# Reordering the joined work of three mixers in a two-block transformer kernel, and computing the memory's row norm once

## The chip, the cores and the metric

One NeuronCore of a Trainium2 chip runs the whole program. The metric is device time in microseconds (us) of one execution, as the median of several. Engines are named as the profile names them: PE is TensorE (its weight loads are PEld), DVE is VectorE, ACT is ScalarE, POOL is GpSimd, and SP issues the weight DMAs.

## The reference

256 tokens of width 1024 go through two blocks one after the other. Cut to what matters here (norm scales, rotary tables and shapes are left out):

```python
# first block: layer 0, then layer 1
x = x + 0.5 * swiglu(rmsnorm(x) , up, down)          # "ffn0"
qkv, z, b, a, rq, rk, rv, rg = split(rmsnorm(x) @ w_in)      # "in0", 14 panels of weights
qkv = silu(causal_depthwise_conv(qkv, conv_w))       # conv, four taps
o = concat(gated_delta_rule(qkv, ...), retention(rq, rk, rv))
x = x + o @ w_out                                    # "out0", then ffn1
x = x + 0.5 * swiglu(...)                            # ffn2
h = rmsnorm(x) @ w_in                                # "in1", 12 panels
o = concat(dilated_attention(4 heads "dil"), softmax(s1) - lam * softmax(s2), 4 heads "dif")
x = x + o @ w_out                                    # "out1", then ffn3, final norm
# second block: two layers l of the same form
for l in range(2):
    kv_m = (rms_norm(mem) * mem_norm_g[l]) @ w_mem_kv[l]     # "mem0", "mem1": same mem in both
    q_a, k_a, v_a, q_h, f_h, i_h, q_m, z = split(rms_norm(x) @ w_in[l])   # "in2_l", 20 panels
    o_a = moba_attention(q_a, k_a, v_a)              # 8 heads "moba"
    o_h = hgrn2(q_h, log_f(f_h), i_h)                # gated recurrence
    o_m = memory_attention(q_m, k_m, v_m)            # 4 heads "matt"
    x = x + (concat(o_a, o_h, o_m) * silu(z)) @ w_out[l]     # "out2_l"
```

## The kernel before

All weights stream through the core once, as panels of 128 x 2048 numbers (1 MB). SP loads panel n into one of three slots of `raw`. ACT copies it, rounded, to `w_hi` (`split_hi(n)`, line 1512) and DVE takes the rest, raw minus `w_hi`, to `w_lo` (`split_lo(n)`, line 1827). PE then multiplies the panel in three products of parts (lines 1010 to 1012), which land in one of two PSUM banks, and an "evacuate" copies them out: on DVE (line 1940) for the first 12 panels of `in0`, else on ACT (line 1612 or 1609). Panel k of an input projection may start when panel k-2 has been evacuated and when its own `split_lo` is done. A slot's `split_hi(n)` waits until PE has used panel n-3.

Every engine works strictly in order. The order is written out by hand: `order()` returns one list of steps (engine, kind, arguments), and each engine runs its own steps of it. `rounds(steps, units)` makes a software pipeline (each step with a lag in rounds), `merge` lays several of them side by side, and `weave(chain, pieces, places)` puts half panels between the rounds at the rounds that a list of places names. In a woven stretch a panel comes as two halves: PE `half(name, k, 0)` and `(name, k, 1)`, ACT `half_hi` (line 1521), DVE `half_lo` (line 1810).

The three places that the change touches:

- First mixer. `in0` panels 0 to 5 feed the convolution. Per panel p: PE product, DVE evacuate, ACT `tap(p)` (line 1629, the first tap), DVE `conv(p-1)` (line 1953, three taps, six instructions), ACT `conv_silu(p-2)` (line 1635), `split_hi` and `split_lo` of the panel three further on. Panel 1 has with it the small products for the gates (`ab_exp`, `softplus`, `g`). Then come the woven rounds of the delta rule: `cumsum`, `gc` (DVE line 1973), `gap` (1980), `decay`, and norms over columns (`cn_sq` on ACT line 1702, `cn_sum` on PE line 1406, `cn_rstd` on ACT line 1710, `cn_use` on DVE line 2078 or 2080). The places are `BESIDE_0`.
- Attention heads. Each head is a pipeline: `scores` on PE (lines 1419, 1421), `mask_max` on DVE (2114), `exp` on ACT (1721), `divide` on DVE (2131, 2135), `turn_p` on PE (transposes, 1431 to 1437), `p_cols` on ACT (1732), `attend` on PE (1377, 1378). `mask_max` of head i waits for `scores(i)` and for `turn_p(i-2)`, whose buffer it writes; `turn_p(i)` waits for `divide(i)`. Two lists fix the order inside a round: `ATTEND_TWO` has `turn_p` ahead of `scores`, `SCORES_FIRST` the reverse. The second mixer (heads dif 0 to 3, dil 0 to 3, woven with `in1` panels 8 to 11) uses the first, the two last mixers use the second.
- Last mixers (`last_mixer(l)`). `f_abs`, `f_ln`, `f_log` and, in layer 1 only, `f_ln2`, `f_log2` (DVE lines 2197, 2198) make the log decay; `k_gate` (ACT 1765) and `cum_f` (DVE 2203) follow, then `diagonal` (PE 1262) and eight levels. Two column norms of the memory keys (`sk`) run beside them. Places are `BESIDE_2`, counted from round n. During layer 0's heads the memory is loaded again (`mem1`), ACT takes its row statistics (`sumsq`, `row_rstd`, lines 1553 to 1561) and DVE scales the rows (`scale`, line 1905).

Of the kernel before, what the change touches and what calls it, by code (L numbers as in the profile page):

```python
# [241 lines left out]
BESIDE_0 = [0, 0, 0, 0, 0, 2, 3, 4, 5, 5, 8, 10, 12, 14, 16, 18]  # L242
# [133 lines left out]
def hgrn_rounds(l):  # L376

    out = [[("dve", "f_abs", (l,)), ("act", "f_ln", (l,))], [("dve", "f_log", (l,))]]
    if l:
        out += [[("act", "f_ln2", (l,)), ("dve", "f_log2", (l,))]]  # L380
    out += [[("act", "k_gate", (l,)), ("dve", "cum_f", (l,))], [("pe", "diagonal", (l,)), ("dve", "diagonal_in", (l,))]]
    ahead = len(out)
    for r in range(8 + 2):
        out.append([(e, k, (l, v)) for e, k, v in
                    [("dve", "gap_f", r), ("act", "decay_f", r), ("dve", "q_level", r - 1), ("pool", "k_level", r - 1),
                     ("pe", "level", r - 2), ("dve", "level_in", r - 2)] if 0 <= v < 8])
    return out + [[("pe", "hgrn_out", (l, g)) for g in (0, 1)]], ahead


def last_mixer(l):  # L390
# [13 lines left out]
    if l == 0:  # L404
        load, *stats = mem_norm(1)
        chains += [[[]] * (h + 1) + [[load]] + [[]] * 3 + [[s for s in stats if s[0] == "act"]] +
                   [[s for s in stats if s[1] == "scale"]]]
    if l:
        chains += [[[]] * (h + 7) + sum(([[("pe", "turn_back", (b,)), ("act", "rows_back", (b,))], []] for b in range(PAIRS)), [])]
    places = [n + r for r in BESIDE_2]  # L410
    out = weave(merge(*chains), halves(panel_list(f"in2_{l}", None, 4)), places)
# [38 lines left out]
def order():  # L450
# [12 lines left out]
    for p, (product, evacuate, *late) in enumerate(panel_list("in0", None, 0, 6)):  # L463
# [3 lines left out]
        out += [evacuate, ("act", "tap", (p,))]  # L467
# [3 lines left out]
        out += [("dve", "conv", (p - 1,))][:p] + ([("act", "conv_silu", (p - 2,))] if p > 1 else []) + late  # L471
    out += [("dve", "conv", (5,)), ("act", "conv_silu", (4,)), ("act", "conv_silu", (5,)), ("act", "logs", ())]
    out += weave(delta_rounds(), halves(panel_list("in0", None, 6)), BESIDE_0)
# [11 lines left out]
    heads = rounds(ATTEND_TWO, [("dif", h) for h in range(4)] + [("dil", h) for h in range(4)])  # L485
# [47 lines left out]
def at(engine, kind, *args):  # L533

    return COUNT_AT[engine, kind, args]


def build(nc, x_in, mem_in, pos_in, panels, gains, small_in, tab0, tab1, tab2, tab3, out):
    with ExitStack() as ctx:
# [1241 lines left out]
        def _(dve):  # L1781
# [121 lines left out]
            def scale(tag, t):  # L1903
                dve.wait_ge(act_done, at("act", "row_rstd", tag, t))
                finish(ts(rows_of(tag)[:, t], rows_of(tag)[:, t], rstd[:, t:t + 1], None, ALU.mult))
# [422 lines left out]
```

## Time and profile before

| | |
|---|---|
| runs | 1621.41, 1624.90, 1620.96 us, median 1621.41 |
| profiled execution | 1623.86 us, of which the span of the trace is 1621.9 |
| PE busy | 1545.7 us, 95% |
| DVE busy | 1177.0 us, 73% |
| ACT busy | 768.9 us, 47% |
| mean granted clock of PE | 0.974 of 2.4 GHz |
| DMA | 246.76 MB, mean 152 GB/s |

How to read it: a timeline row gives the start, the time from start to end, engine, line, operation, output and inputs, and how many instructions of the kind stand there in a row. In square brackets stands how long the engine was idle before the first of them, and which instruction ended that idle time. In windows of time the columns are the stretch, its length, then busy time and count for PE, PEld, DVE, ACT, POOL, then the granted clock as a share of 2.4 GHz, DMA share and GB/s.

### The profile page before, as it was taken

How to read it: one execution, taken by the hardware profiler on the slowest of the kernel's cores; microseconds unless marked ns; L12 is line 12 of the kernel's file. 1: busy time of each engine (PE TensorE's matmuls, PEld its weight loads, DVE VectorE, ACT ScalarE, POOL GpSimd, SP SyncE). 2: the span in 40 equal slices, each digit the busy share in tenths (PEclk: the TensorE clock that was granted, in tenths of full speed). 3: DMA queues.
4: the chain of work that ended last, by engine and by line, in shares of the span. 5: the costliest groups of instructions: out<-in, count | busy, mean ns of one | idle time of the engine just before them, and what ended most of it. 6: DMA issues, size and time to landing. Idle time of an engine off the chain costs nothing.

```text
span 1621.9 us, 23947 instructions
## 1 busy us (share of the span) xinstructions
PE 1545.7 (95%) x9974; PEld 1370.5 (84%) x9974; DVE 1177.0 (73%) x1391; ACT 768.9 (47%) x943; POOL 94.1 (6%) x66
## 2 busy tenths in 40 slices
PE   7999997998999999999997999999999999899998
PEld 6888897887888888888886888888999579799857
DVE  7888667636887788786676787867787565589654
ACT  5333545315433454334535533355646554544653
POOL 1000000010000000000000100001021001013000
PEclk9999999999999999999999999999999789999979
DMA  7555533204555555555431555554443224434202
GB/s 278 201 189 183 179 133 130 79 27 161 204 185 183 185 177 186 203 182 182 173 113 59 202 202 185 182 182 156 156 161 126 78 86 175 156 108 153 104 1 78
DMA packets 51888, 246.76 MB, mean 152 GB/s; under 512 B 4619, under 2 KB 5771, under 8 KB 27718
## 3 DMA queue, kind: packets, MB, share of 16 engines
q1 hardware_dynamic: 50662, 238.29, 42.0%
q0 software_dynamic: 1120, 6.96, 1.2%
q8 instruction: 79, 1.29, 0.3%
q14 instruction: 27, 0.22, 0.0%
HBM read 244.18 MB, written 1.05 MB: 151 GB/s over the span
## 4 chain that ended last, share of the span: by engine, by line
PE 75%; DVE 13%; ACT 6%; issue 3%; DVEq 0%; POOL 0%; ACTq 0%
PE ps L1059 18%; PE ps L1061 9%; PE ps L1010 9%; PE ps L1012 8%; PE ps L1011 8%; PE ps L1111 7%; PE ps L1262 4%; PE ps L1112 4%; DVE w_lo L1827 3%; ACT w_hi L1512 2%; PE ps L1406 1%; DVE act_two L1933 1%; PE ps L1377 1%; ACT act_two L1590 1%; DVE x L1890 1%
## 5 line engine op out<-in xcount | busy, mean ns | idle before, releaser
L1827 DVE TENSOR_TENSOR w_lo<-raw,w_hi 128x2048 fp32r<-128x2048 f32 x188 | 437.2, 2331 | 151.9 <-ACT w_hi L1512 149.3
L1512 ACT ACTIVATE w_hi<-raw 128x2048 fp32r<-128x2048 f32 x188 | 358.9, 1912 | 389.9 <-PE ps L1061 274.9
L1059 PE MATMUL ps<-act_two,w_hi 128*128 128x512 f32 x1408 | 443.9, 397 | 5.0 <-DVE w_lo L1827 2.4
L1010 PE MATMUL ps<-act_two,w_hi 128*128 128x256 f32 x1120 | 331.2, 296 | 18.6 <-DVE act_two L1933 5.4
L1011 PE MATMUL ps<-act_two,w_hi 128*128 128x256 f32 x1120 | 320.0, 286 | 0.0
L1012 PE MATMUL ps<-act_two,w_lo 128*128 128x256 f32 x1120 | 319.9, 286 | 0.0
L1061 PEld LDWEIGHTS ps<-act_two,w_lo 128*128 128x128 f32 x1408 | 264.9, 188 | 62.9
L1061 PE MATMUL ps<-act_two,w_lo 128*128 128x256 f32 x1408 | 277.0, 278 | 0.0
L1010 PEld LDWEIGHTS ps<-act_two,w_hi 128*128 128x128 f32 x1120 | 218.1, 195 | 26.2 <-issue 9.0
L1059 PEld LDWEIGHTS ps<-act_two,w_hi 128*128 128x128 f32 x1408 | 214.9, 189 | 8.0 <-DVE w_lo L1827 3.6
L1011 PEld LDWEIGHTS ps<-act_two,w_hi 128*128 128x128 f32 x1120 | 218.3, 195 | 3.5 <-issue 3.4
L1012 PEld LDWEIGHTS ps<-act_two,w_lo 128*128 128x128 f32 x1120 | 217.9, 195 | 0.0
L1111 PE MATMUL ps<-g_two,w_hi 128*128 128x512 f32 x384 | 136.2, 398 | 0.0
L1810 DVE TENSOR_TENSOR w_lo<-raw,w_hi 128x1024 fp32r<-128x1024 f32 x72 | 98.9, 1403 | 24.2 <-ACT w_hi L1521 23.1
L1111 PE MATMUL ps<-act_two,w_hi 128*128 128x512 f32 x320 | 113.4, 398 | 3.1 <-DVE act_two L1866 2.5
L1112 PE MATMUL ps<-g_two,w_lo 128*128 128x256 f32 x384 | 107.5, 280 | 0.0
L1010 PE MATMUL ps<-w_hi,act_two 128*128 128x256 f32 (+1 forms) x336 | 106.8, 318 | 0.0
L1011 PE MATMUL ps<-w_lo,act_two 128*128 128x256 f32 (+1 forms) x336 | 100.6, 299 | 0.0
L1012 PE MATMUL ps<-w_hi,act_two 128*128 128x256 f32 (+1 forms) x336 | 100.5, 299 | 0.0
L994 POOL TENSOR_TENSOR pair<-pair 128x512 f32<-128x512 f32 x27 | 41.1, 1520 | 872.6 <-ACT pair L1569 871.9
L1112 PE MATMUL ps<-act_two,w_lo 128*128 128x256 f32 x320 | 89.5, 280 | 0.0
L1111 PEld LDWEIGHTS ps<-g_two,w_hi 128*128 128x128 f32 x384 | 72.1, 188 | 16.9
(282 smaller groups left out, 2059.8 us busy)
## 6 DMA issues: line engine op xcount, KB each, us to landing
raw<-panels SPq DMA_DIRECT2D x184, 1024.0 KB, 4.8
raw<-panels SPq DMA_DIRECT2D x80, 512.0 KB, 4.8
raw<-panels SPq DMA_DIRECT2D x8, 256.0 KB, 6.3
table<-tab POOLq DMA_DIRECT2D x1, 1472.0 KB, 9.4
table<-tab POOLq DMA_DIRECT2D x1, 1216.0 KB, 5.6
xn<-x_in SPq DMA_DIRECT2D x4, 256.0 KB, 5.0
work<-mem_in POOLq DMA_DIRECT2D x1, 1024.0 KB, 9.5
xn<-mem_in POOLq DMA_DIRECT2D x1, 1024.0 KB, 5.4
```

The source lines that it names most:

```text
L994: nc.gpsimd.tensor_tensor(pair[:, 0:512], pair[:, 0:512], pair[:, 512 * b:512 * b + 512], ALU.add).then_inc(pool_done, 1)
L1010: pe.matmul(o, l[0], r[0], start=start, stop=False, skip_group_check=shared)
L1011: pe.matmul(o, l[0], r[1], start=False, stop=False, skip_group_check=shared)
L1012: return pe.matmul(o, l[1], r[0], start=False, stop=stop, skip_group_check=shared)
L1059: pe.matmul(grid(ps[:, bank + half], 2), w[half][0], act_two[:, slots[c]], start=c == 0, stop=False)
L1061: ins = pe.matmul(ps[:, bank + half, 0:SEQ], w[half][1], act_hi[:, slots[c]], start=False, stop=c == DC - 1)
L1111: pe.matmul(grid(ps[:, bank], 2), hi, two, start=first and m == 0, stop=False)
L1112: ins = pe.matmul(ps[:, bank, 0:SEQ], lo, two[:, 0], start=False, stop=last and m == len(quarters) - 1)
L1262: ins = pe.transpose(oh, lhs(h), ident) if turn else pe.matmul(oh, lhs(h), rhs(h), start=True, stop=True)
L1512: nc.scalar.activation(w_hi[:, s], raw[:, s], ACT.Copy).then_inc(panel_hi, 1)
L1810: ins = tt(w_lo[:, s, c], raw[:, s, c], w_hi[:, s, c].bitcast(F32), ALU.subtract)
L1827: tt(w_lo[:, s], raw[:, s], w_hi[:, s].bitcast(F32), ALU.subtract).then_inc(panel_lo, 1)
```

## The change

It edits the order of steps and drops some instructions; no product of the reference is computed otherwise.

```diff
-BESIDE_0 = [0, 0, 0, 0, 0, 2, 3, 4, 5, 5, 8, 10, 12, 14, 16, 18]
+BESIDE_0 = [0, 0, 1, 2, 2, 4, 5, 6, 7, 7, 10, 12, 14, 16, 18, 20]
...
     if l:
-        out += [[("act", "f_ln2", (l,)), ("dve", "f_log2", (l,))]]
+        out += [[], [("act", "f_ln2", (l,)), ("dve", "f_log2", (l,))]]
...
     if l == 0:
         load, *stats = mem_norm(1)
-        chains += [[[]] * (h + 1) + [[load]] + [[]] * 3 + [[s for s in stats if s[0] == "act"]] +
-                   [[s for s in stats if s[1] == "scale"]]]
+        chains += [[[]] * (h + 1) + [[load]] + [[]] * 4 + [[s] for s in stats if s[1] == "scale"]]
...
     places = [n + r for r in BESIDE_2]
+    if l:
+        places[:4] = [0, 1, 2, 2]
...
-        out += [evacuate, ("act", "tap", (p,))]
+        his, los = [[x for x in late if x[0] == e] for e in ("act", "dve")]
+        out += [evacuate] + his + [("act", "tap", (p,))]
...
-        out += [("dve", "conv", (p - 1,))][:p] + ([("act", "conv_silu", (p - 2,))] if p > 1 else []) + late
-    out += [("dve", "conv", (5,)), ("act", "conv_silu", (4,)), ("act", "conv_silu", (5,)), ("act", "logs", ())]
-    out += weave(delta_rounds(), halves(panel_list("in0", None, 6)), BESIDE_0)
+        out += [("dve", "conv", (p - 1,))][:p] + ([("act", "conv_silu", (p - 2,))] if p > 1 else []) + los
+    conv_end = [[], [], [("dve", "conv", (5,)), ("act", "conv_silu", (4,)), ("act", "conv_silu", (5,)), ("act", "logs", ())]]
+    out += weave(conv_end + delta_rounds()[1:], halves(panel_list("in0", None, 6)), BESIDE_0)
...
-    heads = rounds(ATTEND_TWO, [("dif", h) for h in range(4)] + [("dil", h) for h in range(4)])
+    heads = rounds(SCORES_FIRST, [("dif", h) for h in range(4)] + [("dil", h) for h in range(4)])
...
             def scale(tag, t):
-                dve.wait_ge(act_done, at("act", "row_rstd", tag, t))
+
+                dve.wait_ge(act_done, at("act", "row_rstd", "mem0", t))
+                dve.wait_ge(loaded[tag], 16)
```

What this does to each engine's own order:

- First mixer, ACT: `split_hi(36)` to `(41)`, six of them, each go ahead of `tap(p)` (and so of `ab_exp`, `softplus` and `conv_silu(p-2)`), and `half_hi(42, 0)` goes ahead of `conv_silu(4)`.
- First mixer, DVE: the evacuation of `in0` panel 6 and `half_lo(42, 0)` go ahead of `conv(5)`.
- Second mixer, PE: `scores` of dif 2, dif 3 and dil 0 to 3, six heads, go ahead of the `turn_p` of the head two before.
- Last mixer of layer 1, PE: `half(in2_1, 4, 0)` goes ahead of the first `cn_sum`. ACT: the evacuation of panel 4 and both `half_hi(207)` go ahead of `f_ln2`, the evacuation of panel 5 and `half_hi(208, 0)` ahead of `k_gate`. DVE: both `half_lo(207)` go ahead of `f_log2`, and `half_lo(208, 0)` ahead of `cum_f`.
- Last mixer of layer 0: `sumsq` and `row_rstd` of `mem1` are gone from ACT (14 records of it in the trace). The two `scale` steps read the root that `mem0` left, and stand in two rounds and no longer in one.

On DVE, at the end of the convolution, the order before (first row: evacuation of panel 5, then `conv(4)`, `split_lo(41)`, `conv(5)`, evacuation of panel 6, halves of panel 42, evacuation of panel 7, halves of 43, `gc`):

```order
L1940 TENSOR_TENSOR work<-ps,r_b 128x2x256
L1953 SCALAR_TENSOR_TENSOR work<-work,small 128x256 x6
L1827 TENSOR_TENSOR w_lo<-raw,w_hi 128x2048
L1953 SCALAR_TENSOR_TENSOR work<-work,small 128x256 x6
L1940 TENSOR_TENSOR work<-ps,r_b 128x512
L1810 TENSOR_TENSOR w_lo<-raw,w_hi 128x1024 x2
L1940 TENSOR_TENSOR work<-ps,r_b 128x512
L1810 TENSOR_TENSOR w_lo<-raw,w_hi 128x1024 x2
L1973 COPY stat<-ps 128x8
```

The same place on DVE with the change (line numbers of the changed file are 2 to 4 higher):

```order
L1944 TENSOR_TENSOR work<-ps,r_b 128x2x256
L1957 SCALAR_TENSOR_TENSOR work<-work,small 128x256 x6
L1829 TENSOR_TENSOR w_lo<-raw,w_hi 128x2048
L1944 TENSOR_TENSOR work<-ps,r_b 128x512
L1812 TENSOR_TENSOR w_lo<-raw,w_hi 128x1024
L1957 SCALAR_TENSOR_TENSOR work<-work,small 128x256 x6
L1812 TENSOR_TENSOR w_lo<-raw,w_hi 128x1024
L1944 TENSOR_TENSOR work<-ps,r_b 128x512
L1812 TENSOR_TENSOR w_lo<-raw,w_hi 128x1024 x2
L1977 COPY stat<-ps 128x8
```

The evacuation of panel 6 and the first half of panel 42 have moved past the last `conv`.

On PE, in the heads of the second mixer, before: after the last product of `half(in1, 9, 1)` come `turn_p` of dif 0 (three transposes), then `scores` of dif 2 (two maps of two products), then the next half panel:

```order
L1012 MATMUL ps<-w_hi,act_two 128x256
L1431 MATMUL ps<-const,work 128x128
L1432 MATMUL ps<-const,work 128x128
L1437 MATMUL ps<-const,work 128x128
L1419 MATMUL ps<-work 128x128
L1421 MATMUL ps<-work 128x256
L1419 MATMUL ps<-work 128x128
L1421 MATMUL ps<-work 128x256
L1010 MATMUL ps<-w_hi,act_two 128x256
```

With the change, at the same place on PE:

```order
L1014 MATMUL ps<-w_hi,act_two 128x256
L1421 MATMUL ps<-work 128x128
L1423 MATMUL ps<-work 128x256
L1421 MATMUL ps<-work 128x128
L1423 MATMUL ps<-work 128x256
L1433 MATMUL ps<-const,work 128x128
L1434 MATMUL ps<-const,work 128x128
L1439 MATMUL ps<-const,work 128x128
L1012 MATMUL ps<-w_hi,act_two 128x256
```

The two steps have changed places, here and at five heads more.

On ACT, in the last mixer of layer 1, before: `cn_rstd` of the second key norm (Ln, Exp), `f_ln2` (Exp, Ln), evacuation of panel 4, halves of 207, `k_gate`, evacuation of panel 5, halves of 208:

```order
L1710 ACTIVATE pair<-ps,const 128x512
L1711 ACTIVATE pair<-pair 128x512
L1760 ACTIVATE work<-work 128x1024
L1761 ACTIVATE work<-work,const 128x1024
L1612 ACTIVATE work<-ps 128x2x256
L1521 ACTIVATE w_hi<-raw 128x1024 x2
L1765 ACTIVATE work<-work 128x1024
L1612 ACTIVATE work<-ps 128x2x256
L1521 ACTIVATE w_hi<-raw 128x1024 x2
```

With the change, from the same `cn_rstd` on ACT:

```order
L1712 ACTIVATE pair<-ps,const 128x512
L1713 ACTIVATE pair<-pair 128x512
L1614 ACTIVATE work<-ps 128x2x256
L1523 ACTIVATE w_hi<-raw 128x1024 x2
L1762 ACTIVATE work<-work 128x1024
L1763 ACTIVATE work<-work,const 128x1024
L1614 ACTIVATE work<-ps 128x2x256
L1523 ACTIVATE w_hi<-raw 128x1024
L1767 ACTIVATE work<-work 128x1024
L1523 ACTIVATE w_hi<-raw 128x1024
```

The evacuation of panel 4 no longer stands behind `f_ln2`, and that of panel 5 not behind `k_gate`.

## Rows read from the trace of the kernel before

**Rows 1.** The page, part 1: busy time of PE.
```profile
PE 1545.7 (95%) x9974; PEld 1370.5 (84%) x9974; DVE 1177.0 (73%) x1391; ACT 768.9 (47%) x943; POOL 94.1 (6%) x66
```
**Rows 2.** Groups of DVE, 232 to 256 us (group, busy, mean ns, idle before it).
```profile
L1827 DVE TENSOR_TENSOR w_lo<-raw,w_hi 128x2048 fp32r<-128x2048 f32 x4 | 9.2, 2292 | 4.6 <-ACT w_hi L1512 4.6
```
**Rows 3.** Timeline of DVE, end of the first mixer's convolution.
```profile
256.36 2.71 DVE L1953 SCALAR_TENSOR_TENSOR work<-work,small 128x256 f32<-128x256 f32 x6
259.11 0.69 DVE L1940 TENSOR_TENSOR work<-ps,r_b 128x512 f32<-128x512 f32 x1
262.30 2.36 DVE L1810 TENSOR_TENSOR w_lo<-raw,w_hi 128x1024 fp32r<-128x1024 f32 x2 [2.50 <-ACT w_hi L1521]
...
267.57 0.16 DVE L1973 COPY stat<-ps 128x8 f32<-128x8 f32 x1
```
**Rows 4.** Timeline of ACT, the three half panels before the first column norm.
```profile
261.14 2.95 ACT L1521 ACTIVATE w_hi<-raw 128x1024 fp32r<-128x1024 f32 x3
```
**Rows 5.** Timeline of PE, first mixer, its two long waits.
```profile
259.85 0.39 PE L1010 MATMUL ps<-act_two,w_hi 128*128 128x256 f32 x1 [3.18 <-DVE work L1940]
...
273.46 1.22 PE L1406 MATMUL ps<-pair,const 128*128 128x512 f32 x1 [4.51 <-ACT pair L1702]
```
**Rows 6.** Timeline of DVE, `mask_max` of dil 1 and dil 2.
```profile
867.98 0.29 DVE L2114 CUSTOM_DVE_ANT_0 work<-ps,table 128x128 f32<-128x128 f32 x1 [1.39 <-PE ps L1421]
...
872.50 0.29 DVE L2114 CUSTOM_DVE_ANT_0 work<-ps,table 128x128 f32<-128x128 f32 x1 [2.40 <-PE ps L1421]
```
**Rows 7.** Timeline of PE, `scores` of dil 2.
```profile
871.54 0.39 PE L1419 MATMUL ps<-work 128*128 128x128 f32 x2
```
**Rows 8.** Timeline of PE, first product of `out1`.
```profile
885.68 0.39 PE L1010 MATMUL ps<-act_two,w_hi 128*128 128x256 f32 x1 [1.48 <-DVE act_two L2071]
```
**Rows 9.** Timeline of ACT, first and last of 14 records of `mem1`'s statistics.
```profile
1292.39 0.63 ACT L1553 ACTIVATE work<-xn 128x512 f32<-128x512 f32 x1
...
1297.24 0.20 ACT L1561 ACTIVATE stat<-stat 128x1 f32<-128x1 f32 x1
```
**Rows 10.** Timeline of DVE, `cn_use` behind them.
```profile
1298.78 0.75 DVE L2078 SCALAR_TENSOR_TENSOR work<-work,small,pair 128x512 f32<-128x512 f32 x1 [6.74 <-ACT pair L1711]
```
**Rows 11.** Timeline of PE, `turn_p` of moba 5, layer 0 and layer 1.
```profile
1301.05 0.48 PE L1431 MATMUL ps<-const,work 128*128 128x128 f32 x1 [1.68 <-DVE work L2131]
...
1565.57 0.47 PE L1431 MATMUL ps<-const,work 128*128 128x128 f32 x1
```
**Rows 12.** Windows of both last mixers.
```profile
1304.00:1308.00 4.00, 4.00 (x16) 2.58 (x15) 1.53 (x8) 1.71 (x7) 0.00 (x0) 0.75 0.00 0
1429.75:1438.23 8.48, 8.48 (x48) 8.48 (x49) 8.38 (x10) 5.29 (x6) 0.00 (x0) 0.65 0.34 122
1439.93:1445.72 5.79, 5.79 (x51) 5.79 (x50) 4.85 (x6) 1.58 (x3) 0.00 (x0) 1.00 0.64 201
1440.00:1540.00 100.00, 100.00 (x796) 95.09 (x796) 81.39 (x87) 52.78 (x66) 19.39 (x8) 1.00 0.39 137
```
**Rows 13.** Timeline of PE, last mixer, layer 1: both `cn_sum`, first products of two halves.
```profile
1411.42 0.84 PE L1406 MATMUL ps<-pair,const 128*128 128x512 f32 x1 [4.43 <-ACT pair L1702]
...
1419.70 1.02 PE L1406 MATMUL ps<-pair,const 128*128 128x512 f32 x2
...
1429.75 0.58 PE L1010 MATMUL ps<-act_two,w_hi 128*128 128x256 f32 x1 [3.29 <-ACT work L1612]
...
1439.93 0.37 PE L1010 MATMUL ps<-act_two,w_hi 128*128 128x256 f32 x1
```
**Rows 14.** Timeline of ACT there: `cn_sq` of the second key norm, `k_gate`.
```profile
1417.02 0.61 ACT L1702 ACTIVATE pair<-work 128x512 f32<-128x512 f32 x1
...
1431.84 1.06 ACT L1765 ACTIVATE work<-work 128x1024 f32<-128x1024 f32 x1 [0.24 <-DVE work L2198]
```
**Rows 15.** Timeline of DVE there: `cn_use`, first half of `f_log2`.
```profile
1426.98 0.75 DVE L2078 SCALAR_TENSOR_TENSOR work<-work,small,pair 128x512 f32<-128x512 f32 x1
1429.32 1.23 DVE L2197 TENSOR_TENSOR work<-work,stat 128x1024 f32<-128x1024 f32 x1 [1.58 <-ACT work L1761]
```

## The prediction

> **What bounds the kernel now.** I read the page's busy times first: PE is busy 95% of the span and every other engine well below it [rows 1]. So a step that moves on DVE or ACT is worth only the PE idle time that it takes away, and PE has about 76 us of it. Then I went through windows and the timeline of PE for its waits near the four places that the diff edits, and from each wait to the engine that ended it. The reader should see, at each place, who comes last: in the first mixer DVE's evacuation and later ACT's norm [rows 5]; at the end of the second mixer the chain of heads, since `out1` can't start before it [rows 8]; in layer 0's last mixer DVE's `divide` [rows 11]; in layer 1's last mixer ACT, twice [rows 13]. Behind the last of these DVE is busy 81 of 100 us and PE all 100 [rows 12], so what PE gains up to there stays gained, and nothing more is won behind it.
>
> **First mixer.** Per panel DVE has conv 2.71, split_lo 2.3 and the evacuation 0.69 [rows 2, 3], 5.7 us, against about 5.8 us of PE products (48 products at full clock took no more than 5.79 in a window [rows 12]). Yet DVE waits 4.6 us in four pieces for `split_hi` [rows 2], which stands behind `tap(p)`, and `tap(p)` waits for DVE's own evacuation. With `split_hi` ahead, these waits go. Against it: `split_hi(37)` now also stands ahead of `ab_exp`, and the first conv starts later: by at least nothing and at most the 1.9 that two halves of a split take on ACT [rows 4]; I take the middle, 1.0, since ACT has idle time there too. So `split_lo(41)`, which ended at 256.36, ends 3.6 earlier, at 252.8. The evacuation of panel 6 comes right there, at 252.9 and no longer at 259.11 [rows 3]: PE's wait of 3.18, which it ended [rows 5], goes in full, since PE was free at 256.67. `conv(5)` has that evacuation (0.7) and a half_lo (1.2) put ahead of it: it starts at 254.8, 1.6 before. Behind its silu ACT has two halves and no longer three before `cn_sq`, 1.0 less [rows 4]: 2.6 earlier. DVE has one half_lo of 1.2 less between `conv(5)` and `gc` [rows 3]: 2.8. What ends PE's second wait (4.51 [rows 5]) comes that much earlier, while that wait keeps its size, for PE arrives earlier too. Behind it PE does the same work. Gain **2.8**; if ACT's silus decide and not the halves, 1.6.
>
> **Second mixer.** In a dil head PE's `scores` take 0.96 us from their start at 871.54 to `mask_max` at 872.50 [rows 6, 7], and they stand behind `turn_p`, which waits for `divide`, which DVE does just ahead of its wait. So they lie on a loop DVE to PE to DVE. DVE waits 1.39, 2.40 and once more 1.39 for them (dil 1 to 3) [rows 6]. With `scores` ahead, `mask_max` waits for `turn_p` alone: 0.9 less each time. But in the 2.40 PE is the late one, with half panels between; it is earlier only by what the loop before gave. I count 0.9 for dil 1, none for dil 2, 0.8 for dil 3: `out1`'s first product, at 885.68 after a wait [rows 8], comes **1.7** earlier. Bounds: 0.8 (one loop) and 2.7 (three). The early heads give nothing: their DVE stands behind half panels.
>
> **Last mixer, layer 0.** The 14 records of statistics hold ACT 5.0 us, 1292.39 to 1297.44 [rows 9]. `cn_rstd` stands behind them, DVE's `cn_use` waits 6.74 for it [rows 10], and PE then 1.68 for `divide` at `turn_p` of moba 5. In layer 1, where ACT has no statistics, the same `turn_p` has no wait [rows 11]. So 1.68 goes; the rest of the 5 us is slack of PE. The clock is 0.75 over 1304 to 1308 [rows 12], so 1.0 us is still lost there. If it rises earlier with the work, up to 1.0 more is won; if it rises when it did, part of the work pulled forward runs at half speed and 0.8 of the gain is lost. Taken **2.0**, range 0.9 to 2.6. Loading and scaling the rows without statistics costs nothing: the two scales stand on DVE before as well.
>
> **Last mixer, layer 1.** PE waits 4.43 before the first `cn_sum` and 3.29 before the next panel's halves [rows 13]. (a) `half(4, 0)`, some 3.1 us (15.04 from 1411.42 to 1426.46 hold four halves and both `cn_sum`), moves into the 4.43. The first `cn_sum` stays, since ACT ends it. The second, at 1419.70, would come at 1416.6, but needs `cn_sq`, which ACT does at 1417.02 to 1417.63 [rows 14]: a new wait of 1.0 to 1.2, gain 2.1. (b) PE is then free at 1424.3 and the next halves' bank, whose evacuation stood behind `f_ln2`, is free by then: no wait of 3.29. They end at 1424.3 + 5.8 = 1430.1 (before, 1438.23). (c) Then comes `diagonal`, which needs the decay. DVE now has two half_lo (2.36 [rows 3]) ahead of `f_log2`: `cn_use` at 1426.98 (0.75), they to 1430.09, `f_log2` with its two halves of 1.23 [rows 15] to 1432.5, against 1431.6 when `k_gate` at 1431.84 had waited 0.24 for it [rows 14]. So `k_gate` ends at 1433.65, 0.7 later, and `diagonal` starts there. The first product behind it, now 1439.93, 1.7 behind `diagonal`'s start at 1438.23, comes at 1435.4: 4.5 earlier. PE has a **new wait of 3.6** before `diagonal`. (d) The clock. Behind the old wait of 3.29 it stood at 0.65 for 8.48 us, and 48 products took 8.48 where 5.79 is the time at 1.00 [rows 12]: 2.7 lost. The new wait of 3.6 may do the same. Behind the 3.18 in the first mixer the first product took 0.39, as in warm stretches, not 0.58 [rows 5, 13]. Waits of one size went both ways, so I take back 1.6, between 0 and 2.7. Gain **2.9**.
>
> On (d), the Trainium skill, "TensorE: Matmul & The Clock Gate", section "HAM oscillation — how this bites in real kernels", says that idle gaps between bursts of matmuls let the clock gate throttle PE again and that each restart costs cold work. The old wait of 3.29 and the 0.65 behind it agree; the 3.18 does not. By the page alone (d) would give 4.5 − 2.7 = 1.8, by the 3.18 row 4.5.
>
> **Sum.** 2.8 + 1.7 + 2.0 + 2.9 = 9.4. The profiled execution took 1623.86 and would become 1614.5. It lies 2.45 above the median of the three runs, so against that median, 1621.41, the time is **1612.0**.
>
> **The rivals.**
> B: both clock terms go the bad way, 1.8 in place of 2.9 and 0.9 to 1.2 in place of 2.0: sum 7.3, 1614.1. For it speaks the old wait of 3.29, against it the 3.18.
> C: no clock is lost behind the new wait (4.5) and the heads of layer 0 bring their 2.6: sum 11.6, 1609.8.
> D: the change doesn't do what it says at two or more places: the late arrivals are replaced by ones just behind them (in the first mixer silu and table load: 1.6; heads 0.8; layer 0 0.9; layer 1, where the 3.6 costs its clock and `k_gate` comes later than I work out, 1): sum 4.3, 1617.1, within 0.3%. Against it: PE's waits of 3.18, 1.68 and 3.29 each have one releaser that plainly moves.
> E, slower. ACT works in order, and `split_hi(36)` to `(41)`, now ahead of `tap`, `ab_exp` and `conv_silu`, must wait for their slot of `raw`, which PE and the load free and fill. In the old order each stood behind a wait for the evacuation, which covered that. If each of six is late, ACT's `tap`, then `conv`, then the next evacuation slip with it. To lose what the rest brings, and to be 0.3% slower, it must cost 14 us, 2.4 per panel. Nothing in the rows shows DVE or ACT waiting for a load there; the four waits of DVE name ACT, not a queue [rows 2].
>
> **How the numbers follow.** 0.3%, 4.9 us, is about what can be told from no change. Chances: forecast (1610.5 to 1613.5) 0.50, B 0.20, C 0.17, D 0.10, E 0.03. B and C are both faster by more than 4.9 us, as is the forecast: faster 0.87; D is the same; E slower. The range runs from 1607.5 (C with the second mixer at 2.7, which is 1608.8, and 1.3 more for the spread of the runs, which is 3.9 from end to end) to 1617.0 (D just reached).
>
> **What would show it.** First mixer: no idle PE before `half(8, 0)`; its later wait still some 4.5, 2.8 earlier; DVE without waits for `split_hi`. If these are there with loads as releasers, E is at work. Second mixer: `mask_max` of the dil heads waits for `turn_p` only. Layer 0: `turn_p` of moba 5 without idle, DVE's wait 6.74 about halved. Layer 1: a short wait before the second `cn_sum`, none before the halves of panel 6, 3.6 before `diagonal`; the granted clock behind it decides between the forecast, B and C. The prediction is wrong if DVE stands at `f_log2` later than 1432.5, if the clock stays down longer than 8.5 us behind the new wait, or if PE's wait in the first mixer only moves from the evacuation to the second one.

## The result, and the profile after

The changed kernel took 1608.06, 1608.75, 1607.84 and 1603.33 us, median 1607.95, against 1621.41 before; the ratio is 0.9907, 95% interval 0.9887 to 0.9926. That is 15 us (12 to 18) faster, where 9.4 were forecast: the direction was right, the size too small. 0.9907 of 1621.41 is 1606.3, below the low end of the range, 1607.5; the plain median, 1607.95, lies just inside it.

The page of the changed kernel, busy times (the same number of products on PE, so less busy time means products at a higher clock):

```profile
PE 1534.8 (96%) x9974; PEld 1364.8 (85%) x9974; DVE 1176.8 (73%) x1391; ACT 765.3 (48%) x929; POOL 94.0 (6%) x66
```

PE is busy 10.9 us less than in [rows 1], in a span that is 16.0 shorter (1605.9). So only 5.1 us came out of PE's idle time, and two thirds came from the same products running faster: the granted clock was low for 84 us of the trace before and for 59 of this one. The forecast was a sum of idle times, with no more than 1.6 us for the clock in any term.

Windows of the changed kernel, then of the one before, cut so that PE has the same work in each (the counts behind PE's busy time agree within 4). The four stretches are all up to the heads of layer 0; those heads; up to the heads of layer 1; the rest:

```profile
0.00:1270.00 1270.00, 1221.69 (x7880) 1094.10 (x7881) 956.61 (x1033) 588.51 (x643) 66.09 (x50) 0.99 0.48 166
1270.00:1320.00 50.00, 44.64 (x224) 30.20 (x224) 32.25 (x103) 29.02 (x74) 0.58 (x1) 0.86 0.13 45
1320.00:1520.00 200.00, 191.44 (x1525) 184.67 (x1523) 142.09 (x143) 108.55 (x129) 25.15 (x11) 0.99 0.42 147
1520.00:1605.00 85.00, 77.05 (x351) 55.84 (x349) 45.83 (x115) 39.22 (x85) 2.23 (x4) 0.90 0.13 50
```
```profile
0.00:1272.00 1272.00, 1221.53 (x7880) 1093.25 (x7881) 956.38 (x1033) 587.96 (x643) 66.12 (x50) 0.99 0.48 166
1272.00:1328.40 56.40, 50.18 (x225) 32.77 (x225) 32.26 (x103) 33.03 (x88) 0.58 (x1) 0.76 0.11 41
1328.40:1531.40 203.00, 192.41 (x1521) 186.42 (x1520) 141.19 (x142) 108.07 (x128) 25.14 (x11) 0.97 0.41 145
1531.40:1621.00 89.60, 81.54 (x354) 58.01 (x352) 47.20 (x116) 39.80 (x85) 2.23 (x4) 0.86 0.13 47
```

The first 1272 us, with the first and second mixer in them, gave 2.0 us; the heads of layer 0, 50 us long, gave 6.4.

The first mixer, DVE of the changed kernel, answering to [rows 3]:

```profile
255.68 2.71 DVE L1957 SCALAR_TENSOR_TENSOR work<-work,small 128x256 f32<-128x256 f32 x6
261.62 1.23 DVE L1812 TENSOR_TENSOR w_lo<-raw,w_hi 128x1024 fp32r<-128x1024 f32 x1 [3.23 <-ACT w_hi L1523]
...
265.76 0.16 DVE L1977 COPY stat<-ps 128x8 f32<-128x8 f32 x1
```

This execution was 0.9 us late before the mixer began (at 200 us it is 0.88 behind, and one stretch of 3.4 us at half clock lies at 27 to 31). So `conv(5)` came at 254.8 and `gc` at 264.9 on the old scale: 2.7 earlier, as worked out. PE's waits there, answering to [rows 5]:

```profile
263.04 1.12 PE L1408 MATMUL ps<-pair,const 128*128 128x512 f32 x2 [1.49 <-ACT pair L1704]
271.65 2.08 PE L1408 MATMUL ps<-pair,const 128*128 128x512 f32 x2 [4.63 <-ACT pair L1704]
```

The wait of 3.18 is gone, one of 1.49 for the column norm stands in its place, and the second keeps its size: 4.51 in the trace before.

`mask_max` of dil 1, 2 and 3 on DVE, answering to [rows 6], and `out1`, answering to [rows 8]:

```profile
867.38 0.29 DVE L2118 CUSTOM_DVE_ANT_0 work<-ps,table 128x128 f32<-128x128 f32 x1 [0.78 <-PE ps L1439]
871.88 0.29 DVE L2118 CUSTOM_DVE_ANT_0 work<-ps,table 128x128 f32<-128x128 f32 x1 [2.40 <-PE ps L1439]
874.77 0.29 DVE L2118 CUSTOM_DVE_ANT_0 work<-ps,table 128x128 f32<-128x128 f32 x1 [0.78 <-PE ps L1439]
```
```profile
884.45 0.56 PE L1012 MATMUL ps<-act_two,w_hi 128*128 128x256 f32 x1 [1.48 <-DVE act_two L2075]
```

They wait for `turn_p` now, 0.6 less at dil 1 and 3 (1.39 before at both) and the same 2.40 at dil 2: `out1` starts 1.23 earlier. At 845 us, ahead of these heads, the two traces stand at the same product at the same time, so the 1.23 is theirs.

The heads of layer 0, PE at `turn_p` of moba 5, answering to [rows 11], and two windows:

```profile
1295.14 0.33 PE L1433 MATMUL ps<-const,work 128*128 128x128 f32 x1 [0.79 <-DVE work L2135]
```
```profile
1277.60:1291.00 13.40, 13.22 (x33) 6.61 (x33) 4.95 (x23) 7.36 (x21) 0.00 (x0) 0.51 0.00 0
1291.00:1305.00 14.00, 13.21 (x64) 8.07 (x64) 9.95 (x39) 9.11 (x27) 0.00 (x0) 1.00 0.00 1
```

And the stretch at half clock of the kernel before:

```profile
1278.80:1305.90 27.10, 24.72 (x63) 12.80 (x62) 10.65 (x44) 16.33 (x50) 0.00 (x0) 0.50 0.03 14
```

Before, 63 products took 24.7 us of PE at 1.2 GHz; now PE is at 2.4 GHz from 1291 on and does 64 in the next 14 us. The prediction had named no idle time at `turn_p` of moba 5; 0.79 is left.

Layer 1's last mixer, PE, answering to [rows 13]:

```profile
1403.07 1.12 PE L1408 MATMUL ps<-pair,const 128*128 128x512 f32 x2 [1.55 <-ACT pair L1704]
1409.33 1.29 PE L1408 MATMUL ps<-pair,const 128*128 128x512 f32 x2 [2.27 <-ACT pair L1704]
...
1425.32 2.05 PE L1264 MATMUL ps<-work 128*128 128x128 f32 x16 [1.85 <-ACT work L1767]
...
1427.12 0.37 PE L1012 MATMUL ps<-act_two,w_hi 128*128 128x256 f32 x1
```

From the first `cn_sum` to the first product behind `diagonal` it is 24.05 us, before 28.51: 4.5 less. `diagonal` itself comes 22.25 behind `cn_sum`; 22.2 had been worked out (1433.65 less 1411.42).

### The profile page after: what moved, and what is told of

It reads as the page before. It is cut to its first block, busy times and chain, and to the rows that moved or that the text cites. A ratio compares the mean times of both kernels' runs of the same rounds, so it can differ in the third digit from the quotient of the medians.

```text
span 1605.9 us, 23931 instructions
## 1 busy us (share of the span) xinstructions
PE 1534.8 (96%) x9974; PEld 1364.8 (85%) x9974; DVE 1176.8 (73%) x1391; ACT 765.3 (48%) x929; POOL 94.0 (6%) x66
## 4 chain that ended last, share of the span: by engine, by line
PE 78%; DVE 13%; ACT 5%; issue 2%; DMA 0%; SPq 0%; DVEq 0%; POOL 0%; ACTq 0%
PE ps L1061 19%; PE ps L1063 10%; PE ps L1012 9%; PE ps L1014 9%; PE ps L1013 9%; PE ps L1113 7%; PE ps L1264 4%; PE ps L1114 4%; DVE w_lo L1829 3%; ACT w_hi L1514 2%; PE ps L1408 1%; DVE act_two L1937 1%; PE ps L1379 1%; ACT act_two L1592 1%; DVE x L1892 1%
## 5 line engine op out<-in xcount | busy, mean ns | idle before, releaser
L1812 DVE TENSOR_TENSOR w_lo<-raw,w_hi 128x1024 fp32r<-128x1024 f32 x72 | 98.7, 1397 | 25.1 <-ACT w_hi L1523 23.9
```

Of the source, the lines that this page charges most:

```text
L1812: ins = tt(w_lo[:, s, c], raw[:, s, c], w_hi[:, s, c].bitcast(F32), ALU.subtract)
```

## The experiments

Two theories. **Idle**: each part gives the idle time that it takes from PE, and the surplus is the clock's chance. **Floor**: the statistics on ACT set a least length for the heads of layer 0, whatever PE's clock did, so that their removal gives the idle time and also makes an early rise of the clock worth something.

Half-clock time below is summed from windows of 1 us of each trace. The kernels were timed in series, each with the kernel before beside them, and means are compared inside a series. Over all 111 executions the kernel before had a mean of 1621.0 us, from 1614.4 to 1626.7, with a standard deviation of 3.3; its means by series ran from 1618.7 to 1622.3. The standard error of a difference of means inside a series is 0.7 to 1.7 us.

**Each part alone, on the kernel before.** The edits are the hunks of the diff: `first_only` has those of `BESIDE_0` and the first mixer, `second_only` this one,

```diff
-    heads = rounds(ATTEND_TWO, [("dif", h) for h in range(4)] + [("dil", h) for h in range(4)])
+    heads = rounds(SCORES_FIRST, [("dif", h) for h in range(4)] + [("dil", h) for h in range(4)])
```

`root_only` those of `mem_norm(1)` and `scale`, `last_only` the round of `f_ln2` and `places`.

first_only: 

> The kernel before with the first mixer's part alone (split_hi ahead of tap, the joined order at the end of the convolution, BESIDE_0). Theory 1, idle time removed: PE's wait of 3.18 us before half(8, 0) goes, the place behind it comes 2.8 to 3.0 us earlier, and the whole kernel is 2.8 us faster (ratio 0.998). Theory 2, clock: of these 3 us about 2 are given back between 340 and 420 us, where the changed kernel had 10.2 us at half clock and the one before 6.8; the whole is 1 us faster (0.9994), and the two long half-clock stretches of the last mixers (27.3 and 23.9 us before) change although nothing of this part stands there.

second_only: 

> The kernel before with the second mixer's part alone (scores ahead of turn_p in six heads). Theory 1: out1 starts 1.2 to 1.7 us earlier, the whole 1.2 to 1.7 faster (ratio 0.999). Theory 2: the same at out1, and then a change of 3 to 7 us in either direction at the last mixers' half-clock stretches, since the work there only falls at another time.

root_only: 

> The kernel before without the second statistics of the memory. Theory 1: PE's 1.68 us wait before turn_p of moba 5 goes, the half-clock stretch there stays about 27 us, gain 1.7 to 2.6 us (ratio 0.9986). Theory 2a, this part itself shortens the stretch: it ends before 1300 us and the gain at that place is 5 to 7 us (0.9965). Theory 2b, the stretch is shorter only because the work before it came 2 us earlier: it stays at 27 us here.

last_only: 

> The kernel before with layer 1's part of the last mixer alone (f_ln2 and f_log2 a round later, first four places 0, 1, 2, 2). Theory 1: the first product behind diagonal comes 2.9 to 4.5 us earlier, nothing is lost to the clock behind the new 3.6 us wait before diagonal, and the whole is 2.9 to 4.5 faster (ratio 0.9977). Theory 2: 4.5 at diagonal, and the stretch at half clock in layer 1's heads (23.9 us before, 17.1 in the changed kernel) is shorter by multiples of about 3.4, each worth 1.7 us, so 4.5 to 8 in all (0.996).

| kernel | ratio (95%) | mean, less the mean before | what its place shows |
|---|---|---|---|
| first_only | 0.9987 (0.9972 to 1.0003) | -2.1 | gc 2.7 earlier |
| second_only | 0.9980 (0.9963 to 0.9997) | -3.6 | out1 1.2 earlier |
| root_only | 0.9953 (0.9930 to 0.9975) | -7.5 | heads of layer 0 3.0 shorter |
| last_only | 0.9969 (0.9953 to 0.9984) | -5.6 | first product behind diagonal 4.5 earlier than before's profile |

At their places the first, second and last part give the same as in the changed kernel. The statistics' part gives the most in the whole (-7.5, standard error 1.7). Its own trace had the clock low for 23.9 us in those heads, so that there theory 2a was not seen and the place gave 3.0, with no wait at `turn_p` of moba 5:

```profile
1298.42 0.47 PE L1430 MATMUL ps<-const,work 128*128 128x128 f32 x1
```

The traces with the statistics show why the mean is larger. `turn_p` of moba 5 in `first_only`, in `second_only` and in `last_only`:

```profile
1298.28 0.48 PE L1432 MATMUL ps<-const,work 128*128 128x128 f32 x1 [6.27 <-DVE work L2132]
```
```profile
1295.67 0.47 PE L1431 MATMUL ps<-const,work 128*128 128x128 f32 x1 [6.58 <-DVE work L2131]
```
```profile
1302.15 0.47 PE L1433 MATMUL ps<-const,work 128*128 128x128 f32 x1 [4.71 <-DVE work L2133]
```

In these three the clock had risen early, at about 1286, 1283 and 1294. The reader is to see the wait: 6.27, 6.58 and 4.71 in place of 1.68 in [rows 11]. From `turn_p` of moba 0 (1275.09, 1272.41, 1278.66; before 1277.56) it is 23.2, 23.3, 23.5 and 23.5 us, nearly the same each time, with PE at 1.2 or at 2.4 GHz; three more traces that kept the single statistics (`half_only`, `round_only`, `stats_back`, below) have 23.2, 23.5 and 23.2. Without the statistics it was 21.7 with the clock low throughout (`root_only`) and 19.6 in the changed kernel. And during the long wait the clock fell again in these three traces, for 6.8 us.

**The statistics put back, doubled in time, and moved.** `stats_back` is the changed kernel with the third part undone. `stats_twice` adds to it eight more sums of squares, 5.0 us of ACT:

```diff
+                if tag == "mem1":
+                    for _ in range(2):
+                        step(nc.scalar.activation(mem_squares[tag][:, 512 * i:512 * i + 512], rows_of(tag)[:, t, c], ACT.Square, accum_out=sumsq[:, i:i + 1]))
```

`stats_spread` is the kernel before, all the work kept, one step in a round:

```diff
-        chains += [[[]] * (h + 1) + [[load]] + [[]] * 3 + [[s for s in stats if s[0] == "act"]] +
-                   [[s for s in stats if s[1] == "scale"]]]
+        chains += [[[]] * (h + 1) + [[load]] + [[]] * 3 + [[s] for s in stats if s[0] == "act"] +
+                   [[s] for s in stats if s[1] == "scale"]]
```

`changed_again` is the changed kernel once more.

changed_again: 

> The changed kernel once more, to have its mean and that of the kernel before over many executions, and a second trace. Both theories: 1605 to 1608 us, ratio 0.991. Clock by chance: the half-clock stretches in the heads of both layers (13.6 and 17.1 us in the first trace) come out differently by multiples of 3.4 us, although the kernel is the same. Clock set by the program: the same stretches again.

stats_back: 

> The changed kernel with the memory's statistics put back into layer 0's heads (the third part undone). Floor theory: with the 14 records on ACT the time from turn_p of moba 0 to turn_p of moba 5 is 23.2 to 23.5 us whatever the clock does (it was in four traces with them; 21.7 and 19.5 in the two without), an early rise of the clock only makes PE's wait there longer (4.7 to 6.6 us) and brings a second drop; the whole is 5 to 7 us slower than the changed kernel. Theory of one wait: only PE's 1.7 us come back, 2 us slower. Clock by chance: no difference beyond 1.7 us in the mean over the runs.

stats_twice: 

> The changed kernel with the statistics put back and each of their four sums of squares taken three times, 8 more ACT instructions of 0.63 us, 5.0 us more in the same place. The output is the same. Floor theory: turn_p of moba 0 to moba 5 takes 28.3 us, 5.0 more than with the single statistics, one for one. If PE at half clock were the bound of that stretch: 5.0 minus what is slack, about 3.

stats_spread: 

> The kernel before with the statistics kept, but spread over six rounds of the heads, one instruction group in each, and the two scales in rounds of their own. Floor theory, place of the work: no long ACT block stands ahead of cn_rstd, the stretch from moba 0 to moba 5 takes 19 to 22 us as without them, and the kernel is as fast as with the statistics dropped (root_only, 0.9953, within 0.002). Theory of the amount of work: only leaving the 5 us of ACT work out helps, and the ratio stays at 0.999 to 1.000.

| kernel | ratio (95%) | mean | moba 0 to moba 5, layer 0 |
|---|---|---|---|
| changed_again | 0.9906 (0.9888 to 0.9924) | 1605.5 | 19.7 |
| stats_back | 0.9953 (0.9935 to 0.9971) | 1613.1 | 23.2 |
| stats_twice | 0.9987 (0.9974 to 1.0001) | 1618.3 | 29.3 |
| stats_spread | 0.9968 (0.9948 to 0.9987) | 1615.2 | 19.7 |

`turn_p` of moba 5 in `stats_back`, `stats_twice` and `stats_spread`:

```profile
1295.50 0.48 PE L1434 MATMUL ps<-const,work 128*128 128x128 f32 x1 [6.34 <-DVE work L2134]
```
```profile
1302.19 0.47 PE L1434 MATMUL ps<-const,work 128*128 128x128 f32 x1 [10.48 <-DVE work L2137]
```
```profile
1296.47 0.33 PE L1431 MATMUL ps<-const,work 128*128 128x128 f32 x1 [0.79 <-DVE work L2131]
```

The floor stands: back, the statistics cost 7.6 us of mean, and the floor is again 23.2. With 5 us more in the same place it is 6.1 longer (a little over one for one), and 5.2 in the mean. Spread out, the same ACT work leaves PE only the 0.79 of the changed kernel: it was the block in one place ahead of `cn_rstd`, not the work. In the whole `stats_spread` is 5.2 faster than the kernel before by means, `root_only` 7.5; the two do not differ beyond their uncertainty. The half-clock stretches of the changed kernel came out as in the first trace (13.6 and 17.1 us), and a third trace, `changed_third` below, has them again. That does not rule out chance: the two traces of one other kernel, `log_first` and `log_first_again` below, have 13.6 and 10.2, then 10.2 and 17.1.

**The last part in pieces.** `half_only` is the kernel before with `places[:4] = [0, 1, 2, 2]` alone, `round_only` with this alone:

```diff
-        out += [[("act", "f_ln2", (l,)), ("dve", "f_log2", (l,))]]
+        out += [[], [("act", "f_ln2", (l,)), ("dve", "f_log2", (l,))]]
```

half_only: 

> The kernel before with the list of places alone changed in layer 1 (half(4, 0) ahead of the first cn_sum), f_ln2 and f_log2 left in their round. Theory, both pieces are needed: the wait of 4.43 us before cn_sum is filled, but the evacuation of panel 4 still stands behind f_ln2 on ACT, so PE's later wait of 3.3 us grows to about 5.5, diagonal starts 26 to 27 us after the first cn_sum as before, gain 0 to 0.5 us. Theory, the filled wait alone is the gain: 2 to 3 us faster.

round_only: 

> The kernel before with f_ln2 and f_log2 alone put a round later, the places unchanged. Theory, both pieces are needed: PE has both cn_sum with no half panel between, so that it waits 4.4 and then up to 5 us for cn_sq, but none for the evacuation of panel 4; diagonal comes 1 to 2 us earlier than before. Theory, the evacuation alone is the gain: 3.3 us faster.

`half_only`: ratio 1.0017 (1.0004 to 1.0030). `round_only`: 0.9996 (0.9985 to 1.0008). PE's wait for the evacuation in the first, and for the second `cn_sq` in the other:

```profile
1429.65 0.58 PE L1012 MATMUL ps<-act_two,w_hi 128*128 128x256 f32 x1 [3.70 <-ACT work L1614]
```
```profile
1418.43 1.22 PE L1406 MATMUL ps<-pair,const 128*128 128x512 f32 x1 [4.50 <-ACT pair L1702]
```

Either piece alone takes one wait and makes another; `diagonal` comes 26.8 and 26.5 us behind the first `cn_sum`, before 26.8. Only together do they give anything; `half_only` is even slower, by 2.0 us in the mean (standard error 0.7).

**Full-size products in the heads.** `fill2` and `fill4` hold half panels of the changed kernel back into the heads:

```diff
-            -1, 0, 1, 2, 3, 4, 5, 6]
+            -1, 0, 1, 2, 3, 4, 7, 8]
```

and `-1, 0, 1, 2, 6, 7, 8, 9]` for `fill4`.

fill2: 

> The changed kernel with the last two half panels of each last mixer held back two rounds, into the first two rounds of the heads. Theory, waits at the head of the heads drop the clock (1.47, 0.94 and 0.81 us within 8 us, then 13 to 17 us at half clock): full-size products between them fill these waits, the half-clock stretches shrink by half or more in both layers, and it is 3 to 8 us faster than the changed kernel. Rival, the small products of the heads hold the clock down whatever stands before them: the same stretches, gain 0 to 2. Rival, the norms that the halves covered now stand bare: 2 to 4 slower.

fill4: 

> The same with the last four half panels held back, to one round ahead of the heads and their first three rounds. Theory of the waits: as fill2 or 1 to 3 us better. Bare norms: 3 to 6 us slower than the changed kernel, since four rounds of norms then have no half panel.

`fill2`: ratio 0.9904 (0.9885 to 0.9924), mean 15.6 below the kernel before beside it, where the changed kernel is 14.2 below in its own series together: 1.4 better with a standard error of 1.6, no gain that can be told. `fill4`: 0.9971 (0.9960 to 0.9982), mean 4.4 below, so some 10 us slower than the changed kernel. In layer 1 the half-clock stretch of `fill2` shrank from 17.1 us to 3.4, all half-clock time from 58 to 32 us (the two other traces of the changed kernel have 49 and 63 in all). In layer 0 it was 10.2 in place of 13.6, which other traces have without the filling. So full-size products between the waits went with a higher clock in layer 1, in one trace; that this pays is not borne out. The rival's waits appeared too, here in `fill4` in layer 0:

```profile
1285.98 0.62 PE L1379 MATMUL ps<-work 128*64 128x256 f32 x2 [2.75 <-ACT work L1614]
```

**Each part left out of the changed kernel, and one step more.** `first_back`, `second_back` and `last_back` undo one part each. `log_first` puts `f_log2` ahead of both `half_lo(207)` on DVE:

```diff
+    if l:
+        i = min(i for i, s in enumerate(out) if s[1] == "half_lo" and s[2][0] == 207)
+        out.insert(i, out.pop(out.index(("dve", "f_log2", (l,)))))
```

first_back: 

> The changed kernel with the first mixer as before. Places theory: 2.7 us slower than the changed kernel, all of it before gc; mean 1608.5 to 1609.5 against 1606. Clock theory: the 3 us shift moves half-clock stretches in or out behind it, any result from 0 to 5 slower.

second_back: 

> The changed kernel with the second mixer's heads as before. Places theory: 1.2 us slower than the changed kernel, at out1. Clock theory: 3 to 4 us slower, as the part alone made the kernel before 3.6 faster in the mean.

last_back: 

> The changed kernel with layer 1's last mixer as before. Places theory: 2.9 us later at the first gap and 4 us later behind the last level, 4 slower in all, 1610; and if more, in the heads of layer 1 that follow, 5 to 6 slower.

log_first: 

> The changed kernel with f_log2 put ahead of both half_lo(207) on DVE. Theory: f_log2 starts when f_ln2 ends, 0.8 us earlier, k_gate and diagonal 0.8 earlier, PE's wait of 1.85 falls to 1.05; the whole 0 to 0.8 us faster than the changed kernel. Rival: half_lo(207), now 3.9 us later, holds up a later load or half panel and nothing is gained, or 1 us lost.

| kernel | ratio (95%) | mean, less the mean before | cost of leaving it out |
|---|---|---|---|
| first_back | 0.9923 (0.9906 to 0.9941) | -12.1 | 2.1 |
| second_back | 0.9931 (0.9913 to 0.9949) | -10.9 | 3.3 |
| last_back | 0.9937 (0.9914 to 0.9959) | -10.1 | 4.1 |
| stats_back, from above | 0.9953 (0.9935 to 0.9971) | -7.4 | 7.6 |
| log_first | 0.9902 (0.9884 to 0.9919) | -15.6 | -1.4 |

The changed kernel is 15.2, 14.9 and 12.8 below the kernel before in its three series, 14.2 by all 16 executions, and the last column is against that (`stats_back` against `changed_again` of its own series). Its standard error is 1.3 to 1.7 us, for `stats_back` 0.8. No changed kernel was timed in the series of the other four, and there the kernel before had its lowest mean, 1618.7; plain differences to the changed kernel's mean of 1606.3 would come out some 2 us smaller (0.3, 1.5, 2.3 and -3.3).

The four left-out parts sum to 17.1 us, the four alone to 18.8, together they are 14.2. Each part has the same order of size both ways, and no pair differs by more than 1.5 us, which is within its uncertainty.

`log_first` did at its place what was worked out:

```profile
1422.20 1.05 PE L1267 MATMUL ps<-work 128*128 128x128 f32 x7 [1.14 <-ACT work L1770]
```

`diagonal` is 0.7 us nearer to the first `cn_sum` (21.5 for 22.25), and the wait 1.14 for 1.85. Beside the changed kernel, in one series:

log_first_again: 

> log_first once more, beside the changed kernel. If its 0.7 us at diagonal is all: its mean is 0 to 1 us below the changed kernel's. If the first comparison holds: 2 to 4 below.

changed_third: 

> The changed kernel, for the comparison with log_first_again in the same call: mean 1605 to 1607 us, and a third trace of its half-clock stretches (13.6 and 17.1 us in the heads in the first two).

`log_first_again`: 0.9917 (0.9896 to 0.9939), mean 1605.9. `changed_third`: 0.9924 (0.9904 to 0.9944), mean 1606.6. The difference is 0.7 us, the size of its place, with a standard error of 0.6. So a gain of 0.7 fits, and none is excluded.

**The places over all traces.** Every trace holds the same 9974 products of PE, so each product of one trace can be found in another and the lag between them followed along the kernel. The table says how much shorter than in the first trace of the kernel before a stretch of products was, in traces with a part and in traces without it (mean, and from least to most; us; the stretches are those of the trace before). Traces in which that place had an edit of its own are left out.

| part | stretch | with it | without it | difference |
|---|---|---|---|---|
| first mixer | 200 to 340 | 3.3 (2.7 to 4.0), 12 traces | 1.2 (0.0 to 2.4), 8 | 2.0 |
| second mixer | 845 to 1000 | 1.7 (1.1 to 3.0), 12 | 0.9 (0.0 to 1.8), 8 | 0.9 |
| no statistics | 1270 to 1328 | 6.3 (2.9 to 7.6), 9 | 0.3 (0.0 to 0.7), 7 | 6.0 |
| last mixer, layer 1 | 1330 to 1460 | 4.3 (3.0 to 4.5), 10 | 1.0 (0.0 to 2.6), 6 | 3.4 |

The third row is the floor once more. Of its seven traces with the statistics, two had the clock low for 27.3 us and five had it rise early, and the stretch was the same to 0.7 us. Of the twelve traces without the block in that place (`fill2`, `fill4` and `stats_spread` too), all but `root_only` had the early rise. The four differences sum to 12.3 us, by standard errors of 0.3 to 0.5 each, against 14.2 in the mean of all executions.

## Why the prediction was wrong

**First mixer, 2.8: right where it was read, less behind it.** Up to the end of PE's second wait it is about 2.7 in every trace that has this part. Of what was named, only the place of PE's remaining wait differs (1.49 before a `cn_sum`). Behind it the gain is 2.0 on average, and some 2 us in the whole (2.1 alone, 2.1 when left out). The cause is the old order: in the first trace the clock stayed up behind the wait of 3.18 and PE then waited 4.51; in the seven other traces of the old order it fell there, and the second wait was 2.2 to 3.0, so that less was lost in total. The clock of the stretch with the 3.18 in it, in the first trace, in `root_only` and in `first_back`, and the second wait in `root_only`:

```profile
255.00:265.00 10.00, 6.82 (x58) 6.61 (x58) 7.39 (x11) 5.87 (x8) 0.00 (x0) 1.00 0.29 107
```
```profile
255.00:265.00 10.00, 6.83 (x45) 6.63 (x44) 7.39 (x11) 6.07 (x8) 0.00 (x0) 0.83 0.31 106
```
```profile
255.00:265.00 10.00, 6.82 (x38) 6.62 (x37) 7.39 (x11) 6.12 (x8) 0.00 (x0) 0.67 0.30 106
```
```profile
273.25 1.25 PE L1405 MATMUL ps<-pair,const 128*128 128x512 f32 x2 [3.02 <-ACT pair L1701]
```

**Second mixer, 1.7: somewhat too large.** 1.2 in place. "I count 0.9 for dil 1, none for dil 2, 0.8 for dil 3": the count of two loops held, but each gave 0.6: the wait for `turn_p` that remains is 0.78, more than the 0.4 which the 0.96 of `scores` leave of the old wait of 1.39. The two steps had overlapped. Over all traces the stretch up to 1000 us is 0.9 shorter with this part.

**Last mixer, layer 0, 2.0: this is the term that failed.** In place 6.4 us. The step reads "The clock is 0.75 over 1304 to 1308, so 1.0 us is still lost there. If it rises earlier with the work, up to 1.0 more is won". The window began too late. The 0.75 was the end of 27.1 us at 0.50, and the whole stretch had to be priced. It also says "the rest of the 5 us is slack of PE". That was so only while PE ran at 1.2 GHz. PE at half clock and ACT's block happened to take nearly the same time, 21.7 against 23.4, so the row with 1.68 showed the difference of two bounds and not the worth of removing one. With PE at 2.4 GHz the floor costs 3.9 at moba 5 (23.5 less 19.6), as the waits of 4.7 to 6.6 us in the traces that kept the statistics show, and a second fall of the clock during that wait. Without the floor the heads were 6 to 8 us shorter in eight traces in which the clock rose early, and 2.9 in the one in which it did not.

**Last mixer, layer 1, 2.9: the clock's term in it was not lost.** In place 4.5, which (a) to (c) had worked out. The 1.6 subtracted in (d) for the clock behind a "**new wait of 3.6** before `diagonal`" was not lost there. The wait was 1.85. The second `cn_sum` waited 2.27 and not 1.0 to 1.2, and the clock fell behind that wait, so that the slow products only took up slack ahead of `diagonal`:

```profile
1410.50:1414.00 3.50, 3.50 (x20) 3.50 (x19) 3.29 (x4) 3.32 (x6) 0.00 (x0) 0.56 0.00 0
```

Rival C's case for this term was the true one in this trace and in ten of the eleven others with this order. In the twelfth, `stats_twice`, what (d) feared did happen: the clock did not fall behind the 2.27, PE waited 3.34 before `diagonal`, the clock fell there, and the first product behind came 25.6 us after the first `cn_sum` in place of 24.05.

```profile
1434.80:1438.20 3.40, 3.17 (x15) 3.17 (x16) 3.37 (x6) 3.40 (x5) 0.00 (x0) 0.50 0.27 106
```
```profile
1435.03 3.57 PE L1265 MATMUL ps<-work 128*128 128x128 f32 x16 [3.34 <-ACT work L1771]
```

So the step that failed in (d) is where the clock would fall, and not that such a wait brings it down. Against other traces of the old order in this place, in which `diagonal` stood 24.2 to 26.7 us behind `cn_sum` and not 26.8, the new order gives 1.9 to 4.4.

Terms in place: 2.7 + 1.2 + 6.4 + 4.5 = 14.8, where 9.4 were summed; layer 0 brought 4.4 more than its term and layer 1 1.6 more, the first two 0.6 less. Of the 16.0 between the two profiles the remaining 1.2 is 3.2 in the heads of layer 1, where nothing was moved (half clock 23.9 us before, 17.1 after), less 0.9 at the start and 1.1 at other places. The stretch had 23.9 there in the profile before, in `half_only` and in `stats_spread`, but 10.2 in `first_only`, `second_only` and `root_only`, so this is not to be credited to the change. The 1.1 is a net figure: between 280 and 845 us the changed kernel gave back 1.7, most of it where its clock was low for 3.4 us longer near 355, and part of that came back later.

**The clock rule.** The clock fell during each long wait at moba 5 (4.71, 6.27, 6.58 us, then 6.8 us low), and in `fill2` the low stretch of layer 1 shrank where full-size products filled waits. The rule of the Trainium skill cited in the prediction ("TensorE: Matmul & The Clock Gate", "HAM oscillation — how this bites in real kernels") agrees with these. The prediction set against it that "the 3.18 does not", and so called the loss in (d) open. That was one trace, an exception: of eight traces with the wait of 3.18, seven had the clock fall between 2.0 and 4.7 us after PE went idle, and of seven with a wait of 3.3 to 3.7 before the next panel's halves, six. Even so what a wait costs could not be read from its length: behind the 2.27 the clock fell in all but `stats_twice` of 13 traces, and it cost nothing in place: `diagonal` came 22.2 us behind the first `cn_sum` with that fall (changed kernel) and without it (`stats_twice`), since PE had slack in between.

**What stays open.** The second mixer's part gained 3.6 alone and cost 3.3 when left out (standard errors 1.2 and 1.5), where its place shows 0.9 to 1.2: both times more, neither time clearly. Why the clock rises early in the heads of layer 0 in most traces, with and without the statistics, and stayed low in two traces that kept them (that of the kernel before and `round_only`) and in `root_only`, no trace shows. What the change is worth without the clock was not measured either, since no run holds the clock.

## What to carry to other kernels

Where PE waits a little for another engine during a stretch at half clock, two bounds lie side by side: ask how long the other engine's chain alone would hold the stretch if PE ran at full clock, and price the removal by that too. Read the granted clock over the whole stretch around a wait, not from where the wait ends. Before one wait is taken as proof that the clock does or does not fall behind it, look at it in more traces: the first trace was here the exception of eight. And put a block of background work on an in-order engine into several rounds: spreading the statistics left PE the same short wait as dropping them.

## What the runs showed of the hardware

PE was busy without a gap from 1279.8 to 1299.4 in the kernel before and stayed at 1.2 GHz all that time, while in the changed kernel it rose to 2.4 GHz after 13.4 us in the same heads: a PE that counts as busy, with the small products of the heads, does not by itself bring the clock back. In the trace of the kernel before, a wait of 3.18 us had no fall of the clock behind it, and in seven other traces the same wait had one. And one kernel, unchanged, spread over 12.3 us in 111 executions with its mean granted clock following the time (0.983 at 1615.3, 0.972 at 1626.4), so that one execution of each kernel could have shown any gain from 6 to 23 us here.
